# Rounded matmuls that walk their columns from the last to the first, with three operand buffers moved by 64 or 128 bytes

## What is computed

```python
def swiglu(h, w_gate, w_up, w_down):
    return (jax.nn.silu(h @ w_gate) * (h @ w_up)) @ w_down

for l in range(2):
    h = rms_norm(x, g_mix[l])
    qa, ka, va, qb, kb, vb, qc, kc, vc, qd, kd, vd, fd = _split_cols(h @ w_in[l])
    ...                                   # four kinds of attention over 256 rows
    x = x + concatenate(groups) @ w_out[l]
    h2 = rms_norm(x, g_ffn[l])
    if l % 2 == 0:
        x = x + swiglu(h2, w_ff_gate, w_ff_up, w_ff_down)
    else:
        x = x + moe_swiglu(h2, w_router, w_exp_gate, w_exp_up, w_exp_down)   # top 2 of 8
```

## Time and profile before

| | us |
|---|---|
| median of 3 runs | 1444.79 (1444.56 to 1445.52) |
| the profiled execution, its own time | 1445.59 |
| its span, first to last instruction | 1443.7 |
| TensorE matmul busy | 1421.5 (98% of the span) |
| VectorE busy | 1119.5 (78%) |
| ScalarE busy | 935.8 (65%) |
| DMA | 301 GB/s over the span, 435.26 MB |

### The profile page before, as it was taken

One profiled execution on the slowest core, in us unless ns is written; L12 is line 12 of the kernel. 1 busy time (PEld: TensorE's weight loads), 2 busy tenths in 40 slices (PEclk: granted clock), 3 DMA queues, 4 the chain that ended last, 5 costly groups with the idle time before them and its releaser, 6 DMA issues.

```text
span 1443.7 us, 16880 instructions
## 1 busy us (share of the span) xinstructions
PE 1421.5 (98%) x6622; PEld 1150.3 (80%) x6622; DVE 1119.5 (78%) x1277; ACT 935.8 (65%) x1234; POOL 82.5 (6%) x102
## 2 busy tenths in 40 slices
PE   7999999999999999999999999999999999999998
PEld 4885888886885778888888888888888888888886
DVE  3565455534566699989998998999999899898996
ACT  4544444424534588777777777777877777777773
POOL 2040000001031010000000000000000000000000
PEclk9999999999999999999999999999999999999999
DMA  9342565435142899999999999999999999999992
GB/s 354 112 143 106 205 234 196 153 136 199 59 151 82 325 394 389 379 385 391 367 379 388 369 378 392 371 373 389 374 372 385 388 364 376 394 379 362 398 377 90
DMA packets 180681, 435.26 MB, mean 301 GB/s; under 512 B 5557, under 2 KB 10357, under 8 KB 180469
## 3 DMA queue, kind: packets, MB, share of 16 engines
q1 hardware_dynamic: 177540, 423.11, 79.0%
q0 software_dynamic: 3056, 11.02, 1.9%
HBM read 428.33 MB, written 5.78 MB: 301 GB/s over the span
## 4 chain that ended last, share of the span: by engine, by line
PE 90%; DVE 4%; ACT 2%; POOL 1%; issue 1%; DMA 1%; SPq 0%; DVEq 0%; ACTq 0%
PE ps L1088 14%; PE ps L1090 14%; PE ps L1089 13%; PE ps L968 8%; PE ps L966 8%; PE ps L967 8%; PE ps L690 4%; PE ps L814 4%; PE ps L942 3%; PE ps L944 3%; PE ps L943 3%; DVE unit_rounded L1921 2%; PE ps L951 2%; PE ps L686 1%; PE ps L688 1%
## 5 line engine op out<-in xcount | busy, mean ns | idle before, releaser
L1921 DVE TENSOR_TENSOR unit_rounded<-wmem,unit_rounded 128x1024 fp32r<-128x1024 f32 (+1 forms) x744 | 854.1, 1210 | 77.5 <-ACT unit_rounded L1381 77.1
L1381 ACT ACTIVATE unit_rounded<-wmem 128x1024 fp32r<-128x1024 f32 (+1 forms) x744 | 719.7, 1043 | 119.8 <-PE ps L1090 59.6
L966 PE MATMUL ps<-unit_rounded,vbuf_rounded 128*128 128x512 f32 x528 | 205.7, 390 | 0.0
L968 PE MATMUL ps<-unit_rounded,stage_rounded 128*128 128x512 f32 x528 | 205.6, 389 | 0.0
L967 PE MATMUL ps<-unit_rounded,vbuf_rounded 128*128 128x512 f32 x528 | 205.4, 389 | 0.0
L1088 PE MATMUL ps<-unit_rounded,qkT_rounded 128*128 128x512 f32 x448 | 177.6, 396 | 0.8 <-DVE qkT_rounded L2084 0.8
L1088 PE MATMUL ps<-unit_rounded,hT_rounded 128*128 128x512 f32 x448 | 177.4, 396 | 0.0
L1090 PE MATMUL ps<-unit_rounded,qkT_rounded 128*128 128x512 f32 x448 | 174.8, 390 | 0.0
L1090 PE MATMUL ps<-unit_rounded,hT_rounded 128*128 128x512 f32 x448 | 174.8, 390 | 0.0
L1089 PE MATMUL ps<-unit_rounded,hT_rounded 128*128 128x512 f32 x448 | 174.5, 389 | 0.0
L1089 PE MATMUL ps<-unit_rounded,qkT_rounded 128*128 128x512 f32 x448 | 174.5, 389 | 0.0
(11 more groups left out here) (239 smaller groups left out, 1526.3 us busy)
## 6 DMA issues: line engine op xcount, KB each, us to landing
wmem<-in_w_exp_gate_dram SPq DMA_DIRECT2D x56, 2048.0 KB, 9.5
wmem<-in_w_exp_up_dram SPq DMA_DIRECT2D x56, 2048.0 KB, 10.0
wmem<-in_w_exp_down_dram SPq DMA_DIRECT2D x56, 2048.0 KB, 9.9
wmem<-in_w_in_dram SPq DMA_DIRECT2D x4, 3072.0 KB, 17.4
wmem<-in_w_ff_up_dram SPq DMA_DIRECT2D x5, 2048.0 KB, 8.9
wmem<-in_w_ff_gate_dram SPq DMA_DIRECT2D x5, 2048.0 KB, 9.1
wmem<-in_w_ff_down_dram SPq DMA_DIRECT2D x5, 2048.0 KB, 7.7
wmem<-in_w_out_dram SPq DMA_DIRECT2D x4, 2048.0 KB, 7.9
```

What stands on the lines that cost most here:

```text
L966: pe.matmul(o, hhb, hi[:, b, c], start=(first and b == 0), stop=False, skip_group_check=True)
L968: mm = pe.matmul(o, hlb, hi[:, b, c], start=False, stop=(b == blocks - 1), skip_group_check=True)
L1381: act.activation(quarter_r(HIGH[l][0 if last else kind], q, cols), quarter(SETS[l][i][kind], q, cols), ACT.Copy).then_inc(hi_ready[kind], 1)
L1921: dve.tensor_tensor(quarter_r(u, q, cols), quarter(u, q, cols), quarter_r(HIGH[l][0 if last else kind], q, cols), ALU.subtract).then_inc(l ...
```

## The change

A helper `from_last` takes the output and the moving operand of a matmul with a step of -1 (`[:, ::-1]`), so that column 511 comes first and column 0 last, in both alike: each column's sum lands where it did. All rounded matmuls go through it. The stationary operand keeps its order.

Besides, two small buffers of 64 bytes (16 floats) are allocated earlier: `ssq` before `qkT`, and `rq0` before `vbuf`. So `qkT` starts 64 bytes, and `vbuf` and `stage` start 128 bytes, behind the place in a 512-byte line at which the moving operands start. `hT` and the stationary operands of `project` keep their place. Nothing else changes: every engine issues the same instructions in the same order, with the same waits.

```diff
@@ -180,7 +180,9 @@
         hT, hT_r = sb_both("hT", [P, KD, T])
+        ssq = sb("ssq", [P, 2, 8])
         qkT, qkT_r = sb_both("qkT", [P, 2, 4, T])
+        rq0 = sb("rq0", [P, 2, 8])
         vbuf, vbuf_r = sb_both("vbuf", [P, 2, NT, GW])
         stage, stage_r = sb_both("stage", [P, NT, 512])
@@ -205,8 +207,6 @@
-        ssq = sb("ssq", [P, 2, 8])
-        rq0 = sb("rq0", [P, 2, 8])
@@ -636,6 +636,10 @@
+            def from_last(out, stationary, moving, start, stop, **kw):
+
+                return pe.matmul(out[:, ::-1], stationary, moving[:, ::-1], start=start, stop=stop, **kw)
+
@@ -1085,9 +1089,9 @@
                     xhk, xlk = xeh_r[e % 2][:, k, :], xel_r[e % 2][:, k, :]
-                    pe.matmul(o, xhk, hi[:, k, :], start=(k == 0), stop=False)
-                    pe.matmul(o, xhk, lo[:, k, :], start=False, stop=False)
-                    mm = pe.matmul(o, xlk, hi[:, k, :], start=False, stop=(k == KD - 1))
+                    from_last(o, xhk, hi[:, k, :], start=(k == 0), stop=False)
+                    from_last(o, xhk, lo[:, k, :], start=False, stop=False)
+                    mm = from_last(o, xlk, hi[:, k, :], start=False, stop=(k == KD - 1))
```

More of the change, by code:

```diff
@@ L685, in project @@
                             xh, xl = [part[l][:, k, t * P:(t + 1) * P] for part in (xs_high, xs_low)]
[L686 to L688 removed]
+                            from_last(pbank(m)[:, 0:cols], xh, high_win[g][:, k, :], start=(k == 0), stop=False)
+                            from_last(pbank(m)[:, 0:cols], xh, low_win[l][g][:, k, 0:cols], start=False, stop=False)
+                            mm = from_last(pbank(m)[:, 0:cols], xl, high_win[g][:, k, :], start=False, stop=(k == KD - 1))
                             continue
@@ L965, in down @@
                         o, c = ps[:, YB[t] + half, :], slice(half * 512, (half + 1) * 512)
-                        pe.matmul(o, hhb, hi[:, b, c], start=(first and b == 0), stop=False, skip_group_check=True)
-                        pe.matmul(o, hhb, lo[:, b, c], start=False, stop=False, skip_group_check=True)
-                        mm = pe.matmul(o, hlb, hi[:, b, c], start=False, stop=(b == blocks - 1), skip_group_check=True)
+                        from_last(o, hhb, hi[:, b, c], start=(first and b == 0), stop=False, skip_group_check=True)
+                        from_last(o, hhb, lo[:, b, c], start=False, stop=False, skip_group_check=True)
+                        mm = from_last(o, hlb, hi[:, b, c], start=False, stop=(b == blocks - 1), skip_group_check=True)
                 if not part_of or blocks - 1 in part_of:
@@ L1104, in last_down @@
                         o, c = ps[:, YB[0] + half, :], slice(half * 512, (half + 1) * 512)
-                        pe.matmul(o, hhb, hi[:, b, c], start=False, stop=False, skip_group_check=True)
-                        pe.matmul(o, hhb, lo[:, b, c], start=False, stop=False, skip_group_check=True)
-                        mm = pe.matmul(o, hlb, hi[:, b, c], start=False, stop=(b == 3), skip_group_check=True)
+                        from_last(o, hhb, hi[:, b, c], start=False, stop=False, skip_group_check=True)
+                        from_last(o, hhb, lo[:, b, c], start=False, stop=False, skip_group_check=True)
+                        mm = from_last(o, hlb, hi[:, b, c], start=False, stop=(b == 3), skip_group_check=True)
                     mm.then_inc(out_full, 1)
```

## The result

| | before | after |
|---|---|---|
| median, us | 1444.82 | 1474.76 (1473.22 to 1475.77) |
| ratio after / before | | 1.0206, 95% interval 1.0188 to 1.0223 |
| span of the profiled execution, us | 1443.7 | 1471.3 |

The prediction, 1408 us and a range from 1393 to 1458, had the wrong sign. The mild form of its third rival (232 ns a matmul, 1472 us) had the size.

The account below looks back on a forecast made before the run. TensorE was taken as the bound; 28 us gained in the expert stage, capped by DMA, plus 7.9 to 11.4 us before it, off 1445.6 us, gave 1406.6 to 1409.7, forecast 1408 us, range 1393 to 1458.

Parts of the forecast that it names:

- third rival: All rounded matmuls: walking down costs time by itself, 1472 us if mild, 2540 us if hard; chance 0.25 for both.
- What bounds the kernel: Whole kernel: TensorE is busy 98% of the span, so a nanosecond per matmul reaches the end almost whole.
- The count and the price of a matmul: 5160 rounded matmuls, 226.7 ns at 512 columns and 120.0 at 256, each with a fixed 13.3 ns, 68.6 us in all.
- the sign against it: Matmuls with 256 columns: spacing must drop as much as with 512; half as much would mean the share isn't fixed.
- A constant cost would not do this: Expert stage: 232 ns behind a break, then 226.7, was taken to show the 13.3 ns as a collision of two streams.
- I take a gain, and near the lower bound: All rounded matmuls: same-direction streams can keep clear of each other, saving up to 10.1 ns each, 13.3 less 3.2.
- The displacement: `qkT` moved 64 bytes, `vbuf` and `stage` 128: changes when the two streams meet in the same part of a line.
- The DMA cap: Expert stage: weight loads allow no step under 16.5 us at 395 GB/s, limiting the gain to 15 to 32 us, 28 taken.
- No change: All rounded matmuls: the 32 cycles belong to the rounded form whatever the read order, 1445 us; chance 0.15.
- Only displaced operands gain: 3336 matmuls with displaced stationary operands gain 10.1 ns, 1412 us, or half, 1428 us; within partial gains, chance 0.20 together.
- Slower: All rounded matmuls: in-place sums or the moving read get slower walking down; mild 5.3 ns each, 1472 us; chance 0.25 including hard.
- The hard case: All rounded matmuls: a second cycle per column, 213 ns each, 2540 us; chance 0.25 together with the mild case.

Follow-up runs that it names:

- e7_sizes: Kernel before, with the experts' gate and up matmuls in 14 forms by turns, 128 to 512 moving and 32 to 128 stationary columns: 1413.86 us.
- e2_place: Kernel before with only the two small buffers moved, matmuls still reading upwards: 1465.09 us, ratio 1.0135.
- e4_places: Kernel before, reading upwards, with gaps putting `hT`, `qkT`, `vbuf` and `stage` 32, 96, 160 and 288 bytes off: 1474.34 us (one run).
- e5_rising: Kernel before, reading upwards, with the moving operand of the experts' gate and up matmuls starting some columns further on, varied over 56 steps: 1456.42 us.

## Why the prediction was wrong, step by step

**What bounds the kernel: right, as far as it was put to the test.** TensorE's busy time grew by 29.6 us and the span by 27.6. No run made the matmuls of 512 columns shorter.

**The count and the price of a matmul: right, the reading of the share only in part.** 5160 matmuls, 226.7 and 120.0 ns. The widths from 256 to 384 and 512 columns in `e7_sizes` have the 13.3 ns again, but only at the common place. I had taken two equal remainders for one fixed share, and had named the sign against it: with 256 columns the spacing should move as with 512. It moved the other way, to 117.8 ns in the changed kernel, 117.8 in `e2_place` and 115.7 in `e4_places`, each time with more at 512.

**"A constant cost would not do this": half right.** The spacing does depend on how the streams stand to each other, as the earlier trace rows suggested, and `e2_place` and `e5_rising` showed it. But the conclusion, that the 13.3 ns are a collision which can be cleared, did not follow. What moves with 512 columns is what comes on top of 226.7 ns: 0 to 13 ns in the sweep of rising walks. Below it nothing was found, in 45 shifts and 56 orders. (With 256 columns part of the share could be cleared, up to 4.3 ns of it.) The rows behind a break should have been read the other way round: 232 ns is what most places had in the sweep, and the steady stream at 226.7 was the case with everything in favour of it.

**"I take a gain, and near the lower bound": the step that failed.** The argument was that two streams with the same direction can keep clear of each other. It put 10.1 ns of gain on a matmul, of which DMA was to leave 7; measured was a loss of 6.7 ns. The falling moving operand costs 233.2 ns or more wherever it stands, and the rising one has a place at which it costs 226.7. I had taken the fixed share of another form of matmul (3.2 ns of the plain one) as the lower bound for this one, though no row showed a rounded matmul under 13.3 ns. That bound was the nearest row, but it was not a row of the same thing, and it should have got a small chance.

**The displacement: not seen as a risk.** The prediction considered only that it may gain. The kernel before kept even its weight windows on multiples of 512 bytes, a layout for which I see no other use in the code; had I priced a loss of 5 ns for the 3336 displaced matmuls, 17 us, it would have been near the 20 us that `e2_place` measured.

**The DMA cap: right in kind, not reached.** I had set a floor of 16.5 us a step at 395 GB/s. In `e7_sizes` DMA moves 393 to 396 GB/s through nearly the whole expert stage, and the 55 steps from the first to the last gate start (481.3 to 1375.0 us) take 16.25 us each. That is 0.25 us less than the floor. Gate loads there land 16.0 us after their issue, against 8.7 in the earlier trace rows, so part of the lead of the loads was spent; whether that is the whole difference isn't shown.

**The rivals.** "No change" by the rule of the Trainium skill, page "TensorE: Matmul & The Clock Gate", section "Step-by-step: what each phase is for", that loading the next stationary operand doesn't take read bandwidth from the running matmul: the measurement speaks against it, as in `e2_place` the spacing hangs on where the stationary operand lies, 233.3 against 226.7 ns. "Slower", mild case: it named the read that no longer runs ahead or the sums as possible mechanisms and 5.3 ns as the price; it was the read, and 6.7 ns; that it no longer runs ahead is not shown. That its 1472 us came within 3 us of the result is in part luck: the price was too low by 1.4 ns a matmul, and the starts of streams lost less than it had put down. "Only displaced operands gain": refuted in both halves. The hard case did not occur.

## What to carry to other kernels

Keep stationary and moving operand of back-to-back `float32r` matmuls of 512 columns at the same place modulo 256 bytes and read the moving one upwards: a stationary operand 64 bytes off, or a falling read, costs 6.7 ns on 226.7 for each matmul. This kernel, bound by TensorE, lost 1.35% by its displaced buffers and 2.0% by the falling read. With 256 columns the same displacement gained 2 ns. A small buffer allocated between two large ones is enough to move an operand so. And when a trace shows two spacings for the same instruction, ask which of them is the rule before costing an edit that is meant to leave it.

## What was not expected of the hardware

- A rounded matmul of 512 columns has a share of 13.3 ns (32 cycles) in a stream, which no order of columns, no place and no narrower stationary operand made smaller. With 256 columns it is no floor: the displacements of `e4_places` brought it down to 9.0 ns. What it consists of stays open.
- A step of -1 or a permuted order of the sums costs nothing; for the read, blocks of 256 bytes may come in any order that was tried, and what happens inside of them counts. Columns falling in groups of 16 cost 266.7 ns, while groups of 4 are free; taking 2 columns in turn from two halves costs 333.3. Why 16 is so much worse than 8 or 32 was not tried further.
- The displacement counts modulo 256 bytes: 256 bytes more on the stationary operand restored the time of before (ratio 1.0002). That it acts through the relation of the two operands is inferred from the displaced stationary operands, which cost what the sweep of the moving one has at the same relative place (233.3 and 233.2, 232.5 and 231.9, 234.3 and 234.1 ns). No run displaced both alike, which would settle it. That the load of the *next* stationary operand is what the moving stream meets is inferred too; no run took the load away.
- The extra cost of falling needs width: none up to 320 columns, 4.6 ns at 384, 6.7 at 512. At 448 the falling share is complete (20 ns), but rising has some of it too. At 256 columns falling is even 1.8 ns faster than rising, which in this kernel concerns 96 matmuls, 0.2 us.
